# Transposing the feed-forward activations with VectorE and DMAs in place of TensorE

## The reference

```
def ffn_sublayer(x, norm_pre, w_gate, w_up, w_down, norm_post):
    h = rms_norm(x, norm_pre)
    y = (jax.nn.silu(h @ w_gate) * (h @ w_up)) @ w_down
    return rms_norm(y, norm_post)
```

## Time and profile before

| | us |
|---|---|
| median of 3 timed runs | 804.0 (803.91 to 804.4) |
| profiled execution, its own time | 804.11 |
| span of its instructions | 802.3 |
| TensorE busy | 794.7 |
| DVE busy | 556.8 |
| ACT busy | 427.5 |
| GpSimd busy | 78.7 |
| DMA, mean rate | 181 GB/s |

### The profile page before, as it was taken

One profiled execution on the slowest core, in us unless ns is written; L12 is line 12 of the kernel. 1 busy time (PEld: TensorE's weight loads), 2 busy tenths in 40 slices (PEclk: granted clock), 3 DMA queues, 4 the chain that ended last, 5 costly groups with the idle time before them and its releaser, 6 DMA issues.

```text
span 802.3 us, 10124 instructions
## 1 busy us (share of the span) xinstructions
PE 794.7 (99%) x3828; PEld 671.7 (84%) x3828; DVE 556.8 (69%) x790; ACT 427.5 (53%) x604; POOL 78.7 (10%) x111
## 2 busy tenths in 40 slices
PE   9999999999999999999999999999999999999997
PEld 7998888888888888888889888888888888888885
DVE  6689999789674555554476979996877655555443
ACT  6587555554554444444475666565536544445431
POOL 1620000122300000000221100002304000000000
PEclk9999999999999999999999999999999999999999
DMA  9675444445575556555355644444563755555531
GB/s 358 220 251 172 146 153 152 157 153 189 178 245 192 184 177 203 168 197 188 129 199 191 214 158 145 144 158 157 167 226 132 259 186 185 183 183 165 205 129 52
DMA packets 41487, 145.47 MB, mean 181 GB/s; under 512 B 4656, under 2 KB 4656, under 8 KB 41440
## 3 DMA queue, kind: packets, MB, share of 16 engines
q1 hardware_dynamic: 41040, 143.15, 52.9%
q0 software_dynamic: 256, 1.16, 0.4%
q10 hardware_dynamic: 144, 0.52, 0.2%
HBM read 143.77 MB, written 1.05 MB: 181 GB/s over the span
## 4 chain that ended last, share of the span: by engine, by line
PE 98%; DMA 1%; ACT 0%; DVE 0%; DVEq 0%; POOLq 0%; issue 0%; SPq 0%; POOL 0%; ACTq 0%
PE acc L397 28%; PE acc L399 27%; PE acc L398 27%; PE acc L516 7%; PE tp L471 4%; PE misc L678 1%; PE tp L696 1%; PE tp L483 1%; DMA gates<-x_cols 1%; PE misc L638 0%; PE tp L654 0%; PE misc L397 0%; PE misc L399 0%; PE misc L398 0%; PE misc L640 0%; ACT w_hi L830 0%
## 5 line engine op out<-in xcount | busy, mean ns | idle before, releaser
L1156 DVE TENSOR_TENSOR w_lo<-raw,w_hi 128x1024 fp32r<-128x1024 f32 (+2 forms) x246 | 300.6, 1229 | 153.4 <-ACT w_hi L830 151.7
L830 ACT ACTIVATE w_hi<-raw 128x1024 fp32r<-128x1024 f32 (+2 forms) x252 | 259.8, 1041 | 197.5 <-PE acc L399 191.3
L397 PE MATMUL acc<-w_hi,xT_hi 128*128 128x512 f32 (+2 forms) x692 | 269.2, 389 | 0.0
L399 PE MATMUL acc<-w_hi,xT_lo 128*128 128x512 f32 (+2 forms) x692 | 265.2, 383 | 0.0
L398 PE MATMUL acc<-w_lo,xT_hi 128*128 128x512 f32 (+2 forms) x692 | 265.0, 383 | 0.0
L399 PEld LDWEIGHTS acc<-w_hi,xT_lo 128*128 128x128 f32 x692 | 129.9, 188 | 24.8
L398 PEld LDWEIGHTS acc<-w_lo,xT_hi 128*128 128x128 f32 x692 | 130.1, 188 | 23.5
L397 PEld LDWEIGHTS acc<-w_hi,xT_hi 128*128 128x128 f32 x692 | 130.1, 188 | 23.4
L397 PE MATMUL acc<-w_hi,hT_hi 128*128 128x512 f32 (+1 forms) x300 | 117.6, 392 | 0.0
L399 PE MATMUL acc<-w_hi,hT_lo 128*128 128x512 f32 (+1 forms) x300 | 116.3, 388 | 0.0
L398 PE MATMUL acc<-w_lo,hT_hi 128*128 128x512 f32 (+1 forms) x300 | 116.2, 387 | 0.0
(11 more groups left out here) (146 smaller groups left out, 631.9 us busy)
## 6 DMA issues: line engine op xcount, KB each, us to landing
raw<-weights SPq DMA_DIRECT2D x247, 512.0 KB, 3.4
raw<-weights SPq DMA_DIRECT2D x14, 384.0 KB, 3.5
raw<-weights SPq DMA_DIRECT2D x8, 288.0 KB, 3.9
gain<-gains SPq DMA_DIRECT2D x4, 512.0 KB, 6.8
x_sb<-x_rows SPq DMA_DIRECT2D x2, 512.0 KB, 9.4
out_rows<-x_sb SPq DMA_DIRECT2D x4, 256.0 KB, 2.1
const<-consts POOLq DMA_DIRECT2D x1, 896.0 KB, 7.9
gates<-x_cols SPq DMA_DIRECT2D x3, 256.0 KB, 7.5
```

Source lines behind the costliest of these rows:

```text
L397: pe.matmul(out, a_hi, b_hi, start=start, stop=False)
L399: return pe.matmul(out, a_lo, b_hi, start=False, stop=stop)
L830: ins = act.activation(w_hi[:, s, first:end], raw[:, s, first:end], ACT.Copy, scale=by)
L1156: ins = dve.tensor_tensor(w_lo[:, s, 0:width], raw[:, s, 0:width], f(w_hi[:, s, 0:width]), ALU.subtract)
```

## The change

`hid` is no longer transposed by TensorE. DVE's `turn` transposes each 32x32 block of it in place of its quadrant of partitions and writes to `turned` (in `gates`, token part 0, which is idle at that time). Sixteen DMAs of SP, `place`, then take 32 partitions x 1 KB each (512 bytes for FL's) from quadrant c of the source to quadrant q of `placed` (in `gates`, token part 1), so that a whole 128x128 block is transposed. ACT's `hi_hidden` copies `placed` to `hT_hi`, DVE's `lo_hidden` subtracts to get `hT_lo`; both read SBUF now where they read PSUM before. `place` of chunk j stands in SP's queue behind the load of unit U_FFN + 8j + 17 (86, 94, 102, 110, 118), and for FL behind that of unit 122, ahead of the loads that follow. In the orders of ACT and DVE the copies of F4 and FL move:

```
+            def place(l, j):
+                sp.wait_ge(turn_done, TOK * (l * CHUNKS + j + 1))
+                if l or j:
+                    sp.wait_ge(hid_lo, TOK * (l * CHUNKS + j))
+                width = (hid_tiles(j).stop - 4 * j) * BLK
+                for q in range(QUADS):
+                    for c in range(QUADS):
+                        src, dst = (gates[BLK * at:BLK * (at + 1), i, D // QUADS * to:D // QUADS * (to + 1)]
+                                    .rearrange("p (t n) -> p t n", t=TOK)[:, :, 0:width]
+                                    for i, at, to in ((0, q, c), (1, c, q)))
+                        sp.dma_start(dst, src).then_inc(place_in, 16)
...
+                    for j in range(CHUNKS):
+                        if u == (U_FFN + 8 * j + 17 if j < FULL_CHUNKS else U_DOWN + 9):
+                            place(l, j)
...
-                def hid_transposes(name, chunk, tiles, bank):
-                    for t in range(TOK):
-                        acc_freed(pe, l, bank + t, chunk)
-                        transposes(TPN[name] + t, [(hid[:, t, c * P:(c + 1) * P], P) for c in range(tiles)])
...
-                    hid_transposes(f"H{2 * (j - 1)}", f"F{j - 1}", 4, 2)
...
-                        hid_transposes("H8", "F4", 4, 2)
...
-                    if i == 2 and t == 0:
-                        hid_transposes("HL0", "FL", 2, 0)
                     if i % 4 == 0:
-                        tp_emptied(pe, l, TPN["H0"] + i // 2 + t)
+                        pe.wait_ge(hid_lo, TOK * (l * CHUNKS + i // 4) + t + 1)
...
+                def hi_hidden(j):
+                    act.wait_ge(place_in, 16 * QUADS * QUADS * (l * CHUNKS + j + 1))
+                    for t in range(TOK):
+                        act.activation(hid_part(hT_hi, j, t), placed_for(j, t), ACT.Copy).then_inc(hid_hi, 1)
...
+                def turn(j, b):
+                    tiles = hid_tiles(j).stop - 4 * j
+                    if l or j:
+                        dve.wait_ge(place_in, 16 * QUADS * QUADS * (l * CHUNKS + j))
+                    for t in range(TOK):
+                        dve.wait_ge(free[b + t], l * FREED[b // 2] + freed(b // 2, f"F{j}" if j < 5 else "FL") + 1)
+                        dve.transpose(turned[:, :, t, 0:tiles, :].rearrange("p q k j -> p k q j"),
+                                      hid[:, t, 0:tiles * P].rearrange("p (k q j) -> p k q j", k=tiles, q=QUADS)
+                                      ).then_inc(turn_done, 1)
+                def lo_hidden(j):
+                    for t in range(TOK):
+                        dve.wait_ge(hid_hi, TOK * (l * CHUNKS + j) + t + 1)
+                        dve.tensor_tensor(hid_part(hT_lo, j, t), placed_for(j, t), f(hid_part(hT_hi, j, t)),
+                                          ALU.subtract).then_inc(hid_lo, 1)
```

More of the change, by code:

```diff
@@ L42 @@
 LAST_W = D_FF - 512 * FULL_CHUNKS
+CHUNKS = FULL_CHUNKS + 1
+BLK = 32
+QUADS = P // BLK
 POOL_LO = {(l, u) for l in range(LAYERS) for u in (U_FFN, U_FFN + 1)}
@@ L88 @@
        "MT0", "MT1", *(f"{piece}{n}" for n in range(8) for piece in "PV"), "O0", "O1",
-       "M0", "M1", "M2", "M3", "F0", "F1", "F2", "F3"] + [f"H{i}" for i in range(10)] + ["HL0", "HL1"])
+       "M0", "M1", "M2", "M3", "F0", "F1", "F2", "F3"])
 TPN = {name: n for n, name in enumerate(TP)}
@@ L207, in build @@
         x_cols = gates[:, :, 2 * D - KD:3 * D]
+        turned, placed = (gates[:, i, 0:D].rearrange("p (q t k j) -> p q t k j", q=QUADS, t=TOK, k=4)
+                          for i in range(2))
         cq = gates[:, :, D:D + Q_RANK + CKV_W]
@@ L254, in build @@
         last_silu = sem("last_silu")
+        turn_done = sem("turn_done")
+        place_in = sem("place_in")
+        hid_hi = sem("hid_hi")
+        hid_lo = sem("hid_lo")
         half_sq = sem("half_sq")
@@ L317, in tp_emptied, with hid_tiles, placed_for, hid_part @@
             eng.wait_ge(tp_free[n % 2], l * (T_USES // 2) + n // 2 + 1)
+        def hid_tiles(j):
+            return slice(4 * j, min(4 * j + 4, FT))
+        def placed_for(j, t):
+            k = hid_tiles(j)
+            return placed[:, :, t, 0:k.stop - k.start, :].rearrange("p q k j -> p k q j")
+        def hid_part(dst, j, t):
+            return dst[:, hid_tiles(j), tokens(t)].rearrange("p k (q j) -> p k q j", q=QUADS)
         def hi_stored(eng, l, n):
@@ L784, in _ @@
                 col_group(U_FFN + 4, 4, 2, 512, 1, "F0", XT, begun=1)
-                def hid_transposes(name, chunk, tiles, bank):
-                    for t in range(TOK):
-                        acc_freed(pe, l, bank + t, chunk)
-                        transposes(TPN[name] + t, [(hid[:, t, c * P:(c + 1) * P], P) for c in range(tiles)])
                 for j in range(1, FULL_CHUNKS):
                     col_group(U_FFN + 8 * j, 4, 2, 512, 0, f"F{j}", XT)
-                    hid_transposes(f"H{2 * (j - 1)}", f"F{j - 1}", 4, 2)
                     col_group(U_FFN + 8 * j + 4, 4, 2, 512, 1, f"F{j}", XT)
-                def last_beside(i):
-                    if i == 2:
-                        hid_transposes("H8", "F4", 4, 2)
-                col_group(U_LAST, 4, 2, 2 * LAST_W, 0, "FL", XT, beside=last_beside)
+                col_group(U_LAST, 4, 2, 2 * LAST_W, 0, "FL", XT)
                 def down_waits(i, t):
-                    if i == 2 and t == 0:
-                        hid_transposes("HL0", "FL", 2, 0)
                     if i % 4 == 0:
-                        tp_emptied(pe, l, TPN["H0"] + i // 2 + t)
+                        pe.wait_ge(hid_lo, TOK * (l * CHUNKS + i // 4) + t + 1)
                 wide_group(U_DOWN, FT, "DOWN", HT, down_waits,
@@ L1084, in _ @@
                                        ).then_inc(free[t], 1)
-                    for t in range(TOK):
-                        hi_T(f"H{2 * (j - 1) + t}", hT_hi[:, 4 * (j - 1):4 * j, tokens(t)])
+                    hi_hidden(j - 1)
                     his(U_FFN + 8 * j + 8, U_FFN + 8 * j + 12)
[L1089 to L1092, removed]
+                his(113, 117)
+                hi_hidden(4)
                 for t in range(TOK):
@@ L1098, in _ @@
                 act.preload_act_table(ACT.Sigmoid)
[L1099 to L1102, removed]
+                his(117, 124)
+                hi_hidden(5)
+                his(124, 135)
             wide_square(LAYERS - 1, R_DOWN, 0, "DOWN")
@@ L1446, in _ @@
                 los(74, 81)
+                def turn(j, b):
[12 more added lines that the diff above has]
+                                          ALU.subtract).then_inc(hid_lo, 1)
                 def hidden(t, use):
                     bank(2 + t, use)
+                    if l or use != "F0":
+                        dve.wait_ge(turn_done, TOK * (l * CHUNKS + int(use[1])))
                     acc_freed(dve, l, t, use)
@@ L1457, in _ @@
                     hidden(t, "F0")
+                turn(0, 2)
                 for j in range(1, FULL_CHUNKS):
                     los(U_FFN + 8 * j + 4, U_FFN + 8 * j + 8)
-                    for t in range(TOK):
-                        k = slice(4 * (j - 1), 4 * j)
-                        lo_T(f"H{2 * (j - 1) + t}", hT_lo[:, k, tokens(t)], hT_hi[:, k, tokens(t)])
+                    lo_hidden(j - 1)
                     los(U_FFN + 8 * j + 8, U_FFN + 8 * j + 12)
@@ L1465, in _ @@
                         hidden(t, f"F{j}")
[L1466 to L1469, removed]
+                    turn(j, 2)
+                los(113, 117)
+                lo_hidden(4)
+                dve.wait_ge(turn_done, TOK * (l * CHUNKS + 5))
                 for t in range(TOK):
@@ L1475, in _ @@
                                              op0=ALU.mult, op1=ALU.mult).then_inc(free[t], 1)
[L1476 to L1479, removed]
+                turn(5, 0)
+                los(117, 124)
+                lo_hidden(5)
+                los(124, 135)
             for t in range(TOK):
```

## The result

The changed kernel takes 813.87 us (median of 4 runs, 813.66 to 815.28) against 804.11 for the kernel before on the same chip: a ratio of 1.0124, 95% interval 1.0108 to 1.014. It is slower by 9.8 us, where 4.5 us faster was forecast, and 813.87 lies outside the stated range. The difference is clear of noise. The profiled execution took 813.96, with a span of 812.2.

A forecast was written before the change was run, and what follows sets the result against it. The prediction took TensorE, busy 794.7 of 802.3 us, as the bound. Removed transposes (-9.9) and two new waits (+5.4) summed to -4.5 us, giving 799.5 us against the 804.0 median, range 796.0 to 803.2.

The forecast's parts named there:

- What the transposes cost: On TensorE, removing 88 transposes of hid was to save 4.96 us a layer, 9.9 us in two layers.
- Where the new wait stands: In DOWN's second pass, TensorE was to wait 2.7 us a layer for FL's evacuation, 5.4 us in all.
- The issue pitch, 0.47 us: On SP, back-to-back placing DMAs were to start 0.47 us apart, so a piece of sixteen takes 7.5 us.
- the upper end of 0.58: Upper bound of SP's pitch, the longest weight issue; it was to add 3.3 us for both layers.
- the case for a lower pitch: Rival: a pitch of 0.29 to 0.33 us lands placement early, TensorE never waits, 794.1 us; chance 0.13.
- In the chunks 0 to 3 all of this hides: Placement, copies and held weight loads were to be covered there, with 4.8 us to spare before TensorE wants the next unit.
- `lo_hidden`, which ends some 6 us before its next `hidden`: In chunks 0 to 3, the only DVE wait that placement lengthens, claimed to have some 6 us of room.
- a pitch of 0.80: The SP issue cost in us at and above which the next chunk's w_hi was also to start being late.
- The rest of the sum: Before FL's wait: 2.1 us landing, 1.40 for two turns, then copies, Silus and hidden until TensorE resumes.
- The clock: Rival: TensorE's clock falls in the 2.7 us wait, costing 5.4 to 16.3 us, 804.9 us taken; chance 0.07.
- SP as the bound: Rival: slower DMA issues on SP lengthen the wait; at 0.75 us each, 807.9 us; chance 0.11.
- threshold of 0.62: SP pitch in us beyond which a layer's FL wait passes the 4.96 us saved and the change stops paying.

The follow-up runs named there:

- fl_first: Changed kernel with FL's evacuation (Silu, table load, hidden) and unit 117 done ahead of chunk 4's copies on ACT and DVE; 795.07 us.
- probe: Kernel before, plus groups of DMAs of several forms at the placements' spots in SP's queue, their data used by no engine; 804.18 us against 804.14.
- pool_queue: Changed kernel with the sixteen placing DMAs issued from GpSimd's queue in place of SP's; 809.35 us.
- last_eight: Changed kernel with sixteen placing DMAs in chunks 0 to 3 but only eight in chunk 4 and FL, half of their blocks left out; 802.79 us.
- filler: Changed kernel with 32 unused 512-column matmuls added on TensorE ahead of the first matmul that waits for FL; 810.74 us.
- bounce: Changed kernel with each piece sent through a DRAM scratch tensor, four DMAs writing and one reading back, in place of sixteen direct DMAs; 797.38 us.
- fl_pool: Changed kernel with FL evacuated ahead of chunk 4's copies and the sixteen placing DMAs issued from GpSimd's queue; 795.78 us.
- no_drift: Changed kernel with eight placing DMAs in chunks 0 to 3, half of their blocks left out, and all sixteen in chunk 4 and FL; 806.73 us.
- late_copies: Changed kernel with the copies of chunks 0 to 3 on ACT and DVE moved behind the next four weight units; 818.02 us.
- both_orders: Changed kernel with copies of chunks 0 to 3 behind four weight units and FL evacuated ahead of chunk 4's copies; 799.97 us.

## Why the prediction was wrong, point by point

Two steps failed, the price of an issue and the cover of the chunks 0 to 3, and a term that the sum had left to a rival, the clock, came with them.

- **What the transposes cost: right.** 9.9 us forecast; 804.18 - 794.30 = 9.88 and 804.13 - 794.13 = 10.0 measured.
- **Where the new wait stands: right**, and the only one that is new in TensorE's stream. fl_first shows it: with FL first it goes.
- **The issue pitch, 0.47 us: failed, and with it the upper end of 0.58.** I took it from rows whose DMAs read DRAM and gave it to DMAs with SBUF on both sides. Measured: 0.64 in the last chunk, so the sixteenth issue starts 9.6 us after the first and not 7.05, +2.6 a layer. Partition count, on which I had built the case for a lower pitch, does not enter (probe).
- **"In the chunks 0 to 3 all of this hides": failed.** I counted what TensorE has to spare and not whether DVE comes back in time. "`lo_hidden`, which ends some 6 us before its next `hidden`" left out the four `w_lo` that stand between them (4.63 us). With 22.2 us or more for a round against 21.76, lateness adds up: +3.7 a layer at F4. A round less its issues is 22.2 - 10.0 = 12.2 us, so the loop takes longer than a chunk from a pitch of (21.76 - 12.2) / 16 = 0.60 on. That is just above the range that I had given, to 0.58: at the forecast's pitch this step would have held, as layer 0 of pool_queue shows at 0.49. The limit itself was missing; I had put the first effect on the next chunk at a pitch of 0.80.
- **The rest of the sum: right.** From `hidden` to the first issue 4.2 us (4.5 forecast), landing 1.9 (2.1), turns 1.29 a pair (1.40), from the landing to TensorE's start 2.89 (2.85). So 2.7 + 2.6 + 3.7 - 0.5 (these small ones) - 0.3 (TensorE came 0.3 later than the formula) = 8.2, against 8.15.
- **The clock: a rival at 0.07 that came true beside the forecast.** I priced it at a lost 5.4 us; it cost 3.75. I gave it a small chance as an event by itself, although the forecast's own wait was of a length for which the trace had no row. A wait of 3.1 us was enough in pool_queue and one of 2.7 in last_eight, so the forecast's own 2.7 a layer would not have been safe either. The page "TensorE: Matmul & The Clock Gate" of the Trainium skill (Part 1) has an idle array put back to the lower clock; the window after the wait agrees (0.52), and so does the filler run, where the matmuls behind it keep their full pace.
- **SP as the bound: near, by other means.** Its threshold of 0.62 for "slower" lies below the measured 0.64, but that alone gives a wait of 5.25 us a layer, 10.5 in all against 9.9 saved: 0.6 us slower. The other 9 us are the loop and the clock, which this rival did not have, so that it names the right side is in part luck. I had set the threshold just above the longest issue of the trace and gave the case 0.11. The page "DMA: Bandwidth & Descriptors" of the Trainium skill (Rules for kernel authors), that transfers under 64 KB are mostly overhead, is borne out: 512 KB in sixteen pieces cost SP 10 us, and the five larger transfers of bounce did better even through DRAM.

Open: why an issue with SBUF on both sides takes longer; why some take 1.2 to 1.9 us; why a DMA that GpSimd issues lands later in layer 1 (5.4 us) than in layer 0 (3.9); and what besides its length decides whether a wait brings the clock down.

## What to carry to other kernels

When a transfer's completion is put ahead of other work in an in-order queue, ask first what stands behind it that does not need it: moving FL's evacuation ahead of the copies was worth 18.8 us, more than any quicker transfer of the same blocks (16.5 by way of DRAM). When a step hands its result from chunk to chunk over several queues, add up the whole round, with every instruction that stands between, and compare it with the chunk's time; slack on the bounding engine says nothing about a loop that does not pass it. Take an issue's price from a DMA with the same two sides, and if none is in the trace, count it as unknown well beyond the longest row.

## What the runs showed of the hardware that I had not expected

- SP's issue of a DMA with SBUF on both sides has a median of 0.59 us (0.63 to 0.71 apart in a row), of one that reads DRAM 0.42 (0.47 apart); 16, 32 or 128 partitions, 256 bytes to 2 KB make no difference (probe). GpSimd issues the former 0.49 apart, but they land 3.5 us after their issue (median), where SP's land after 1.9, and its drain at the end of the program takes 5.9 us in place of 1.0 (pool_queue, fl_pool).
- VectorE turns the 32x32 blocks of a 128x512 float32 tile in 0.65 us (1.29 a pair), the time of the subtract of that size.
- In the profiled executions TensorE's granted clock fell to its lower level after each wait for FL of 1.8 us and more (bounce, last_eight, pool_queue, no_drift, the changed kernel, late_copies) and not after one of 1.3 (bounce) or 0.7 (filler); some 6 to 10 matmuls in a row then start 0.43 us apart. The length alone does not decide: after TensorE's wait of 2.3 us for a `w_lo` in both_orders the clock stayed at 1.00.
